# mLSTM iterations with two blocks of 12 projection matmuls in place of three, and the sample's products with its old state in spare columns of a projection bank

## What is computed

```python
def _mlstm(q, k, v, i_pre, logf, C0, n0, m0):
    ...
    def step(carry, xs):
        C, n, m = carry
        ...
        S = jnp.einsum('bhtd,bhsd->bhts', qc, kc) * Dm
        g = jnp.exp(b + m[..., None] - m_t)
        num = jnp.einsum('bhts,bhsv->bhtv', S, vc) + g[..., None] * jnp.einsum('bhtd,bhdv->bhtv', qc, C)
        den = jnp.sum(S, axis=-1) + g * jnp.einsum('bhtd,bhd->bht', qc, n)
        h = num / jnp.maximum(jnp.abs(den), jnp.exp(-m_t))[..., None]
        ...
        C_new = decay[..., None, None] * C + jnp.einsum('bhs,bhsd,bhsv->bhdv', w, kc, vc)
```

## Time and profile before

| | us |
|---|---|
| median of 3 runs (574.04 to 574.15) | 574.13 |
| the profiled execution | 574.21 |
| its span, first to last instruction | 572.4 |
| the mLSTM iterations in it | 273.9 to 376.8 |
| TensorE busy with matmuls | 562.4 (98%) |
| VectorE, ScalarE, GpSimd busy | 263.9, 204.2, 134.2 |

### The profile page before, as it was taken

One profiled execution on the slowest core, in us unless ns is written; L12 is line 12 of the kernel. 1 busy time (PEld: TensorE's weight loads), 2 busy tenths in 40 slices (PEclk: granted clock), 3 DMA queues, 4 the chain that ended last, 5 costly groups with the idle time before them and its releaser, 6 DMA issues.

```text
span 572.4 us, 9946 instructions
## 1 busy us (share of the span) xinstructions
PE 562.4 (98%) x4039; PEld 519.9 (91%) x4039; DVE 263.9 (46%) x536; ACT 204.2 (36%) x548; POOL 134.2 (23%) x140
## 2 busy tenths in 40 slices
PE   8999999999999999999999999999999999999996
PEld 7999999999899999999988889899999998888874
DVE  5620011584566556511476768446534537052223
ACT  6842211413544444410546454234332225011011
POOL 1101122122143324412012121236424430011001
PEclk9999999999999999999999999999999999999999
DMA  8752210812111011107023230411113325044231
GB/s 314 288 195 75 65 38 3 283 55 82 38 40 38 1 38 40 38 12 176 2 68 116 75 93 21 111 45 66 39 38 82 102 74 183 1 147 148 100 102 56
DMA packets 32037, 49.93 MB, mean 87 GB/s; under 512 B 4508, under 2 KB 23196, under 8 KB 31976
## 3 DMA queue, kind: packets, MB, share of 16 engines
q1 hardware_dynamic: 31560, 48.77, 26.7%
q10 hardware_dynamic: 432, 0.53, 0.3%
HBM read 41.70 MB, written 8.05 MB: 87 GB/s over the span
## 4 chain that ended last, share of the span: by engine, by line
PE 94%; DVE 2%; issue 1%; DMA 1%; ACT 1%; POOL 1%; DVEq 0%; POOLq 0%; ACTq 0%
PE ps L579 51%; PE ps L517 9%; PE ps L518 8%; PE ps L519 8%; PE ps L631 2%; PE ps L691 2%; PE ps L756 1%; PE ps L732 1%; PE ps L768 1%; PE ps L654 1%; PE ps L522 1%; PE ps L521 1%; PE ps L697 1%; PE ps L758 1%; DMA w_raw<-in_w_in_tiles 1%
## 5 line engine op out<-in xcount | busy, mean ns | idle before, releaser
L579 PE MATMUL ps<-x_hl,w_hi 128*128 128x364 f32 (+1 forms) x1200 | 303.0, 332 | 1.6 <-DVE x_hl L1156 1.0
L579 PEld LDWEIGHTS ps<-x_hl,w_hi 128*128 128x128 f32 x1200 | 211.1, 188 | 9.2 <-issue 6.1
L579 PE MATMUL ps<-x_hl,w_lo 128*128 128x364 f32 (+1 forms) x600 | 197.8, 330 | 0.0
L579 PEld LDWEIGHTS ps<-x_hl,w_lo 128*128 128x128 f32 x600 | 112.8, 188 | 0.1
L1642 POOL TENSOR_TENSOR qmT<-qmT,sg 128x364 f32<-128x364 f32 (+1 forms) x24 | 33.8, 1407 | 51.1 <-DVE sg L1492 30.4
L997 ACT ACTIVATE prob<-prob,nmx 128x192 f32<-128x192 f32 (+1 forms) x64 | 27.9, 437 | 45.9 <-DVE sd L1304 45.9
L517 PE MATMUL ps<-wt_hi,x_hl 128*128 128x324 f32 x128 | 39.9, 312 | 0.0
L519 PE MATMUL ps<-wt_hi,x_hl 128*128 128x324 f32 x128 | 39.8, 311 | 0.0
L518 PE MATMUL ps<-wt_lo,x_hl 128*128 128x324 f32 x128 | 39.8, 311 | 0.0
L1594 POOL TENSOR_TENSOR prob<-prob,rden 128x768 f32<-128x768 f32 (+1 forms) x16 | 22.6, 1415 | 72.2 <-DVE rden L1310 72.2
L336 POOL TENSOR_TENSOR w_lo<-w_raw,w_hi 128x1024 fp32r<-128x1024 f32 x12 | 28.8, 2401 | 42.5 <-ACT w_hi L920 42.5
(11 more groups left out here) (241 smaller groups left out, 901.4 us busy)
## 6 DMA issues: line engine op xcount, KB each, us to landing
w_raw<-in_w_in_tiles SPq DMA_DIRECT2D x24, 512.0 KB, 3.6
x_tok<-in_x_prompt SPq DMA_DIRECT2D x8, 512.0 KB, 4.6
w_raw<-in_w_out_tiles SPq DMA_DIRECT2D x8, 512.0 KB, 3.5
x_res<-in_x_prompt SPq DMA_DIRECT2D x8, 512.0 KB, 4.1
out_y_prompt<-y_out SPq DMA_DIRECT2D x7, 512.0 KB, 2.9
wt_raw<-in_w_tok SPq DMA_DIRECT2D x4, 648.0 KB, 7.7
logw<-lw_rows SPq DMA_DIRECT2D x8, 256.0 KB, 4.1
Cs<-in_state_C SPq DMA_DIRECT2D x16, 128.0 KB, 2.4
```

Source lines behind the costliest of these rows:

```text
L579: last = mm(ps[:, sub_bank(sub), 0:w], wt, xm, start=(at_ == 0), stop=(at_ == 23))
```

## The change

TensorE's iteration becomes two blocks of 12 projection matmuls: one between `state_update` and `m_scores`, one behind `k_transposes`. `sample_round` follows on `sample_inter` with no projection between them. `h_transposes(0)` moves ahead of `m_scores`' place in `it` = 11. The products of `sample_inter(r)` go into columns 364 to 492 of the projection bank that sub `S_P3` + r has used. They therefore wait for that sub's evacuation and no longer for `st_done`; `sample_round` keeps `st_done` and no longer waits for `it_evac`; the projection that takes the bank again, two subs later, waits for `it_evac`.

```diff
-    IT0 = 320
+    IT0 = 364
+
+    def inter_bank(r):
+
+        return sub_bank(S_P3 + r)
...
                         wait(pe, "proj_free", sub - 1)
+                    if S_P3 + 2 <= sub < S_P3 + 2 + N_ROUND:
+                        wait(pe, "it_evac", sub - S_P3 - 1)
...
         def sample_inter(r):
             h, q = r // 2, r % 2
-            wait(pe, "st_done", r)
+            wait(pe, "proj_free", S_P3 + r + 1)
...
-                last = mm(ps[PQ * c:PQ * (c + 1), 4, IT0:IT0 + W1], qmT[:, h, T_P + PQ * half:T_P + PQ * (half + 1)],
+                last = mm(ps[PQ * c:PQ * (c + 1), inter_bank(r), IT0:IT0 + W1], qmT[:, h, T_P + PQ * half:T_P + PQ * (half + 1)],
...
         def sample_round(r):
             h, q = r // 2, r % 2
             wait(pe, "st_done", r)
-            wait(pe, "it_evac", r + 1)
...
-            project(7)
+            project(12)
             if it == NC + 2:
                 h_transposes(NC, it)
                 numerator(0)
+            if it == NC + 3:
+                h_transposes(0, it)
             if it <= NC:
                 m_scores(it)
             if 1 <= it <= N_ROUND:
                 sample_inter(it - 1)
-            project(7)
-            if it == NC + 3:
-                h_transposes(0, it)
-            if 1 <= it <= N_ROUND:
                 sample_round(it - 1)
             if it <= NC:
                 k_transposes(it)
-            project(10)
+            project(12)
```

More of the change, by code:

```diff
@@ L1088, in _ @@
                 wait(act, "it_done", it)
-                A_(ITs[:, it // 2, :], ps[:, 4, IT0:IT0 + W1], ACT.Copy, scale=inter_msk[:, 0:1]).then_inc(s("it_evac"), 1)
+                A_(ITs[:, it // 2, :], ps[:, inter_bank(it - 1), IT0:IT0 + W1], ACT.Copy, scale=inter_msk[:, 0:1]).then_inc(s("it_evac"), 1)
             if it <= NC:
@@ L1401, in inter_second @@
             part = ITs[:, r // 2, :]
-            STT(out=part, in0=ps[:, 4, IT0:IT0 + W1], scalar=inter_msk[:, 1:2], in1=part, op0=ALU.mult, op1=ALU.add)\
+            STT(out=part, in0=ps[:, inter_bank(r), IT0:IT0 + W1], scalar=inter_msk[:, 1:2], in1=part, op0=ALU.mult, op1=ALU.add)\
                 .then_inc(s("it_evac"), 1)
```

## The result

The changed kernel takes 577.4 us (577.26 to 577.6), the kernel before 574.14 (574.04 to 574.24), four runs each: a ratio of 1.0057 with a 95% interval of 1.0045 to 1.0069. It is slower by 3.3 us; 577.5 was forecast. The profiled execution took 577.6 us, of which 575.8 is span, 3.4 more than before.

What follows compares the result with a forecast made beforehand. TensorE bounds the kernel, but in even iterations its wait on the path from `sample_inter` over `inter_second` to `sd_mul` sets the length. Terms from +1.39 through `it` = 2 to +0.20 in 11 sum to +3.36: 577.5 us, range 576.2 to 578.5.

Steps and rivals of the forecast that it cites:

- The slot: One projection matmul takes 0.166 us; five more ahead of `sample_inter` lengthen `it` = 2, 4, 6, 8 by 0.83 each.
- The chain: Even iterations: `sample_inter` through `inter_second` and `sd_mul` to `h_transposes`; time to `sample_inter` plus 4.7 us sets their length.
- The switch: TensorE leaving projections and coming back: 0.15 us (0 to 0.20) saved in each of `it` = 0, 1, 3, 5, 7.
- The stall in `it` = 2: `state_update` waits for the copy into `n_s`: a new 0.86 us stall, +1.39 us by the iteration's end.
- Iteration 5: `sample_inter`'s 0.27 us wait for `Cst` goes; with the saved projection border, -0.42 us.
- Iterations 3, 5 and 7 keep their cover: Odd iterations: `d_exp` ends 0.83 us later, which just fits before `sd_mul`, so they do not lengthen.
- The tail: `it` = 11: `h_transposes(0)` has 24 slots behind the numerator in place of 31 and waits 0.2 us for `h_scale(0)`.
- the matmul row by itself: TensorE's busy row, 9.78 of 9.78 us in `it` = 7, would leave nothing to save: sum 0.75 us higher.
- the first case: Whole kernel as forecast: 576.9 to 578.3 us, ends from a border saving of 0.20 or none; chance 0.70.
- the signs: Profile after: `h_transposes` idle 1.2 to 1.4 us, iterations 4, 6, 8 at 11.0 to 11.2, `state_update` stall 0.7 to 0.9.
- the one without the stall: Even iterations lengthen but `state_update` in `it` = 2 does not wait: 0.86 us less, 576.6 us; chance 0.12.
- faster: Products in their own bank free the even iterations, which `inter_second` does not set: 573.1 us; chance 0.07.

Runs made afterwards that it cites:

- The sizes 7, 12 and 17: First block of 7 or 17 projections (second block 17 or 7) against the changed kernel's 12 and 12: 573.12 and 585.53 us, against 577.4.
- The first experiment: Changed kernel with VectorE's `inter_second` moved from ahead of `h_mean_square` to behind `sd_mul`: 571.21 us, ratio 0.9953 to the kernel before.
- the last two runs on VectorE's moves: Changed kernel, `inter_second` behind `sd_mul`, with `w_lo` behind `sample_state` (570.65 us) or between `h_mean_square` and `h_scale` (571.71 us).

## Why the prediction was right

- **The slot.** 0.166 us each, five of them: the even iterations grew by 0.83, 0.83 and 0.80. The sizes 7, 12 and 17 lie on that slope in all but the clock, with even iterations of 10.35, 11.18 and 12.03 us.
- **The chain.** It was read from two things, VectorE's idle ahead of `inter_second` and the 4.59 us from there to `h_transposes`. The first experiment confirms both: with that instruction out of the chain the even iterations are TensorE's. The prediction's 4.7 us count from the end of `sample_inter`; from its start to `h_transposes` are 5.08 us before and 5.09 after, and no term of the sum uses them.
- **The switch.** Taken as 0.15 (0 to 0.20). Iterations 3 and 7 saved 0.18 each (9.63 against the 9.81 between 294.81 and 304.62 of the trace before, 9.60 against 9.78), so the border between the two small groups costs next to nothing. Iteration 0 saved only some 0.04: `m_scores` of `it` = 1 went from 280.27 to 281.13, which is 0.86 later, where the slots are 0.83 and the trace was 0.07 late before the mLSTM part.
- **The stall in `it` = 2.** The copy into `n_s` was forecast to end at 287.07; it starts then and ends at 287.24, and `state_update` starts at 287.39 where 287.22 was forecast. These 0.17 us are the 0.07 from ahead of the mLSTM part and iteration 0's smaller saving. The idle of 0.74 lies in the range of 0.7 to 0.9. By the first matmul of `it` = 3 the kernel was 1.66 us late (296.47 against 294.81) where 1.39 was forecast. Of the other 0.1, 0.07 passed between `state_update` and the projection behind it (0.88 us after the stall, 0.81 before the change).
- **Iteration 5.** -0.53 measured, -0.42 forecast. The wait for `Cst` held TensorE for more than its 0.27 of idle, since what is shown as idle starts after a matmul's whole way: in the run with blocks of 7, 7 and 10, where that wait is gone and the switches stay, iteration 5 is 0.38 us shorter (10.01 against 10.39).
- **Iterations 3, 5 and 7 keep their cover**, as forecast: no idle in front of `h_transposes` in 4, 6 and 8. With five slots more it was used up, and still cost only 0.20 us in iterations 3 and 7.
- **The tail.** `h_transposes(0)` starts at 375.70, right behind `h_scale(0)`, which ends at 375.64. It stands for some 0.15 us (0.20 was forecast), too short to be shown as idle.
- **Two slips that the forecast survived.** Only four savings can reach the end, since that of iteration 1 goes into the stall. So the matmul row by itself would have raised the sum by 0.60 us and not 0.75, and the first case runs from 577.1 to 578.1, not from 576.9 to 578.3. Of the signs, the first wait before `h_transposes` was 1.48 us (1.2 to 1.4 forecast) and iteration 8 took 10.93 us (11.0 to 11.2).
- **The size of the misses.** +0.27 by the end of iteration 2, -0.03 in each of iterations 3, 7 and 8, -0.11 in iteration 5 and some -0.06 in the tail cancel nearly, which is luck: the sum was 3.36 and the profiled execution shows 3.4, but no single term beyond the slot is known to better than 0.1.

Of the rivals, the one without the stall is refuted by the row of `state_update`, and "faster" by the 6.5 us of idle at `inter_second`. It has a true core, though: the spare columns do open a faster kernel, but only once VectorE's order is changed with them.

## What to carry to other kernels

Before matmuls are regrouped to save switches, look at what each small group starts on another engine: a projection slot moved ahead of a product that another engine waits for costs its full length in each iteration in which the way back from that engine sets the end, and here this was four times 0.83 us against switches of 0.18. A reader of results that nobody needs soon (here `inter_second`) belongs behind the work that the next iteration waits for, and a place of its own for the results is what permits it. An idle stretch of an engine that waits for its neighbour is not free room if both use the same path to memory.

## What the runs showed of the hardware

Idle stretches of TensorE of 2.0 to 2.4 us in an otherwise busy stretch were followed, in two of the four cases in the run with blocks of 17 and 7 (after 2.26 and 2.03 us) and in two of the three of the run with `inter_second` moved in the kernel before (after 2.19 and 2.42 us), by a granted clock of 0.50 (the 1.2 GHz level) for some 3 us. Each such drop cost about 1.3 to 1.7 us. After the other three, of 2.31, 2.25 and 2.22 us, the clock stayed at 1.00, so the length of the idle alone doesn't decide it, and what does stays open. After the idle stretches of 1.2 to 1.5 us in the changed kernel the clock stayed at 1.00. I had not counted on this, and it is the greater part of why two of the expectations were too low.

VectorE and GpSimd slow each other down in both directions: GpSimd's `TENSOR_SCALAR` on 4 columns took 1.14 us beside VectorE's `w_lo` in place of 0.23, and VectorE's `q_gate` 1.25 us in place of 0.68 while GpSimd wrote `vmk` (the rows stand with the last two runs on VectorE's moves).
